# Feature pieces of a three-product matmul: heads and tails of the tokens as one moving operand of 512 columns, the halves of the bank added at the eviction

## The chip, the cores and the metric

The kernel runs on one core of a Trainium2 chip. The metric is the device time of one execution in microseconds. Three executions of the kernel before took 2441.64, 2445.85 and 2447.97 us; the median is 2445.85.

## The reference

All values are fp32. A sequence of 256 tokens with 2048 features goes through two blocks. The first block has two layers; in each, the normalized tokens are projected by one wide matrix, and the columns feed three kinds of attention (A: 6 heads with a decay, B: 6 heads through a low rank, C: 4 heads that take the difference of two softmaxes), whose gated outputs are projected back and added:

```python
for l in range(DEPTH):                       # 2 layers
    h = _rms_norm(x, norm_g[l])
    proj = jnp.einsum('bsd,dn->bsn', h, w_in[l])
    (a_q, a_k, a_v, a_f, a_gate, b_cq, b_ckv, b_krope, b_gate,
     c_q, c_k, c_v, c_gate) = jnp.split(proj, IN_OFFSETS, axis=-1)
    a_out = _fox_attention(...) * jax.nn.silu(a_gate)
    b_out = _mla_attention(...) * jax.nn.silu(b_gate)
    c_out = ... * jax.nn.silu(c_gate)
    mixed = jnp.concatenate([a_out, b_out, c_out], axis=-1)
    x = x + jnp.einsum('bsm,md->bsd', mixed, w_out[l])
```

The second block modulates and normalizes the tokens, runs two banded attentions with 64-wide heads (`proj = h @ w_in[l]`, split into qa, ka, va, qb, kb, vb), projects back, and ends with a mixture of 32 experts that runs all experts' weights past the tokens.

## The kernel before, in words

**Weights.** The weights of the first block and of the second block's attention come in pieces of 1 MB (128 x 2048 fp32), through a ring of 5 raw buffers loaded by SP. Each piece is split in halves of 1024 columns: ScalarE rounds a half to the fp32r format (`w_head`, L778, L1659), VectorE subtracts it from the raw half to get the rest (`w_tail`, L1175, L1889). There are 3 split buffers, and both splits run two pieces ahead (AHEAD = 2). The tokens are split in the same way into `h_head` and `h_tail`, 16 tiles of 128 features x 256 tokens each. A product is the sum of three matmuls, head x head, head x tail, tail x head (`three`, L945 and L1776).

**Pieces.** A layer of the first block has 73 pieces: 16 token pieces (out: tokens x 512 features, the tokens stationary, 512 columns moving), then 18 feature pieces of the A heads (query, key, gate of each of 6 heads), the feature piece of the rotary key (`kr`), 4 pieces of the low-rank projections (`low`, `lowv`), 6 feature pieces for the B gates, 12 for the C heads (query, key, gate), 16 output pieces. A feature piece (L1001, L1802) has the weights stationary (16 tiles of 128 x 128) and the 256 tokens moving, so 48 matmuls of 256 columns into one PSUM bank, of which the columns 0 to 255 are used. There are 37 such pieces in a layer and 26 in the second block (2 `ka`, 8 each of `qa`, `qb`, `kb`), so 100 in all.

**Order.** Each engine walks one list of steps, in strict order (`layer_schedule`, `second_schedule`); a piece is followed by steps due a number of pieces later. After an A key come its score and softmax, one piece later the transposes of the probabilities (`turn`), two pieces later the product with the values (`value`). After a B gate piece come the score of that B head, the gate and the softmax; after a C key two scores. In the second block the score follows `qa` (A part) or `kb` (B part), and the value step of the head before stands between the piece and the score. TensorE's score waits until the query and key of its head are evicted.

**Evictions.** In the first block VectorE evicts queries, keys and the rotary key: one instruction multiplies the bank by the tokens' reciprocal norms `rrow` (L1223 with a scale, L1226). For a gate VectorE multiplies (L1241), clamps (L1242), ScalarE takes exp, ln, exp (L875 to L877), and VectorE multiplies the result with the clamped value (L1246). In VectorE's order a gate of a B head stands after the reduction of the score (L1325 to L1332) and before its softmax (L1338 to L1341); in ScalarE's order it stands after the exponentials of the score (L902, L904). In the second block ScalarE evicts the feature pieces with one copy (L1707). 

**Beside it.** VectorE also sums the modulation weights (`ada`, L1262, 128 x 2048, about 2.35 us each), one after each of 16 in 18 pieces of a layer, and splits the mixed rows before the output pieces (L1386). Every wait is a counted semaphore; `chain.link` lets an instruction wait for the one before it on its own engine.

## Time and profile before

| | |
|---|---|
| median of three runs | 2445.85 us (2441.64 to 2447.97) |
| the profiled execution | 2444.84 us |
| its span, first to last instruction | 2442.7 us |
| mean granted TensorE clock | 0.977 of full speed |
| TensorE busy (matmuls) | 2222.4 us |
| VectorE busy | 1388.2 us |
| ScalarE busy | 732.9 us |
| HBM read | 757.28 MB, 311 GB/s over the span |

The rows below come from one profiled execution. A row of the timeline gives the start in us from the beginning of the span, the duration, the engine, the line of the kernel, the operation, what it writes and reads, its shape, and how many instructions the row holds. A bracket gives the idle time of the engine just before and the instruction that ended it; "issue" there means that the profile shows no releaser. PE is TensorE, PEld its weight load, DVE VectorE, ACT ScalarE. Matmuls are pipelined: their recorded durations overlap, so the distance between starts tells the pace. The first layer of the first block spans about 60 to 500 us, its A heads 136 to 264, B heads 288 to 355, C heads 355 to 443; the second layer repeats it about 500 us later; the feature pieces of the second block lie between 1062 and 1317 us, and the experts come after.

### The profile page before, as it was taken

How to read it: one execution, taken by the hardware profiler on the slowest of the kernel's cores; microseconds unless marked ns; L12 is line 12 of the kernel's file. 1: busy time of each engine (PE TensorE's matmuls, PEld its weight loads, DVE VectorE, ACT ScalarE, POOL GpSimd, SP SyncE). 2: the span in 40 equal slices, each digit the busy share in tenths (PEclk: the TensorE clock that was granted, in tenths of full speed). 3: DMA queues.
4: the chain of work that ended last, by engine and by line, in shares of the span. 5: the costliest groups of instructions: out<-in, count | busy, mean ns of one | idle time of the engine just before them, and what ended most of it. 6: DMA issues, size and time to landing. Idle time of an engine off the chain costs nothing. (4 is left out here: it accounts for less than half of the span.)

```text
span 2442.7 us, 37024 instructions
## 1 busy us (share of the span) xinstructions
PE 2222.4 (91%) x14593; PEld 1639.7 (67%) x14593; DVE 1388.2 (57%) x2051; ACT 732.9 (30%) x1343; POOL 43.0 (2%) x61
## 2 busy tenths in 40 slices
PE   6999999999999989979999978998888888888886
PEld 5899988788899888778898864444444444444442
DVE  6877788887787888666454634333333333333334
ACT  5444444454435434356554422000000000000001
POOL 0100000000000000030000000000000000000000
PEclk9999999999999999989999979999999999999998
DMA  8877766788777567674344256999999999999997
GB/s 320 322 298 292 275 242 247 307 314 338 293 295 274 224 260 265 246 269 148 147 141 152 105 227 245 422 422 422 422 422 422 422 422 422 422 422 422 422 422 322
DMA packets 108686, 761.77 MB, mean 312 GB/s; under 512 B 12288, under 2 KB 15392, under 8 KB 16800
## 3 DMA queue, kind: packets, MB, share of 16 engines
q1 hardware_dynamic: 108432, 759.49, 78.3%
q8 instruction: 73, 1.20, 0.2%
q10 hardware_dynamic: 144, 0.79, 0.1%
q14 instruction: 37, 0.30, 0.0%
HBM read 757.28 MB, written 2.95 MB: 311 GB/s over the span
## 5 line engine op out<-in xcount | busy, mean ns | idle before, releaser
L2312 PE MATMUL b_ps<-s_raw,s_window 128*64 128x256 f32 x4096 | 461.2, 382 | 58.2 <-DVE x_tokens L2538 39.3
L2312 PEld LDWEIGHTS b_ps<-s_raw,s_window 128*64 128x64 f32 x4096 | 295.6, 137 | 235.4 <-issue 72.6
L1175 DVE TENSOR_TENSOR s_w_tail<-s_raw,s_w_head 128x1024 fp32r<-128x1024 f32 x292 | 344.9, 1223 | 39.1 <-ACT s_w_head L778 39.0
L947 PE MATMUL b_ps<-s_h_head,s_w_head 128*128 128x256 f32 x1184 | 346.1, 292 | 0.0
L948 PE MATMUL b_ps<-s_h_tail,s_w_head 128*128 128x256 f32 x1184 | 339.1, 286 | 0.0
L949 PE MATMUL b_ps<-s_h_head,s_w_tail 128*128 128x256 f32 x1184 | 338.7, 286 | 0.0
L778 ACT ACTIVATE s_w_head<-s_raw 128x1024 fp32r<-128x1024 f32 x292 | 293.0, 1049 | 102.3 <-DMA s_raw<-in_w 70.6
L1262 DVE SCALAR_TENSOR_TENSOR s_ada_acc<-s_raw,s_c_col,s_ada_acc 128x2048 f32<-128x2048 f32 x120 | 282.3, 2352 | 0.0
L2332 PE MATMUL b_ps<-s_raw,s_diag 128*64 128x512 f32 x1024 | 237.8, 600 | 39.2 <-DMA s_raw<-in_w_down 24.0
L947 PEld LDWEIGHTS b_ps<-s_h_head,s_w_head 128*128 128x128 f32 x1184 | 231.1, 195 | 12.9 <-issue 9.4
L948 PEld LDWEIGHTS b_ps<-s_h_tail,s_w_head 128*128 128x128 f32 x1184 | 231.3, 195 | 0.2
L949 PEld LDWEIGHTS b_ps<-s_h_head,s_w_tail 128*128 128x128 f32 x1184 | 231.1, 195 | 0.0
L2220 ACT ACTIVATE s_hidden<-b_ps 128x256 f32<-128x256 f32 x32 | 12.3, 384 | 644.3 <-PE b_ps L2312 644.3
L2332 PEld LDWEIGHTS b_ps<-s_raw,s_diag 128*64 128x64 f32 x1024 | 66.1, 136 | 190.3 <-issue 84.8
L2530 DVE TENSOR_TENSOR s_y<-b_ps,s_gate_row 128x512 f32<-128x512 f32 x64 | 44.3, 692 | 237.4 <-PE b_ps L2332 237.4
L2538 DVE TENSOR_TENSOR x_tokens<-b_ps,x_tokens 128x1024 f32<-128x1024 f32 x128 | 147.8, 1217 | 32.5 <-PE b_ps L2347 32.5
L947 PE MATMUL b_ps<-s_w_head,s_h_head 128*128 128x512 f32 x416 | 164.2, 395 | 0.0
L949 PE MATMUL b_ps<-s_w_head,s_h_tail 128*128 128x512 f32 x416 | 162.8, 391 | 0.0
L948 PE MATMUL b_ps<-s_w_tail,s_h_head 128*128 128x512 f32 x416 | 162.8, 391 | 0.0
L1889 DVE TENSOR_TENSOR s_w_tail<-s_raw,s_w_head 128x1024 fp32r<-128x1024 f32 x104 | 126.3, 1253 | 54.1 <-ACT s_w_head L1659 53.9
L1778 PE MATMUL b_ps<-s_h_head,s_w_head 128*128 128x256 f32 x416 | 119.7, 288 | 0.9 <-ACT s_v L1697 0.9
L2516 DVE TENSOR_SCALAR s_hidden<-s_hidden 128x256 f32<-128x256 f32 x32 | 9.4, 294 | 193.1 <-ACT s_hidden L2220 193.1
(336 smaller groups left out, 3147.8 us busy)
## 6 DMA issues: line engine op xcount, KB each, us to landing
s_raw<-in_w SPq DMA_DIRECT2D x198, 1024.0 KB, 5.1
s_raw<-in_w_ada SPq DMA_DIRECT2D x128, 1024.0 KB, 5.2
s_raw<-in_w_gate SPq DMA_DIRECT2D x128, 1024.0 KB, 24.1
s_raw<-in_w_up SPq DMA_DIRECT2D x128, 1024.0 KB, 26.5
s_raw<-in_w_down SPq DMA_DIRECT2D x128, 1024.0 KB, 26.5
x_tokens<-in_x SPq DMA_DIRECT2D x1, 2048.0 KB, 7.8
s_rel<-in_rel SPq DMA_DIRECT2D x1, 2048.0 KB, 11.6
s_raw<-mod_rows SPq DMA_DIRECT2D x2, 1024.0 KB, 12.3
```

The source lines that it names most:

```text
L778: act.activation(w_head[:, g % SPLITS, cols], raw[:, ring, cols], ACT.Copy)\
L947: pe.matmul(out, head, m_head, start=first, stop=False, skip_group_check=True)
L948: pe.matmul(out, head, m_tail, start=False, stop=False, skip_group_check=True)
L949: return pe.matmul(out, tail, m_head, start=False, stop=last, skip_group_check=True)
L1175: dve.tensor_tensor(w_tail[:, g % SPLITS, cols], raw[:, slot["w", g], cols], w_head[:, g % SPLITS, cols].bitcast(F32), ALU.subtract)\
L1262: ins = dve.scalar_tensor_tensor(out=ada_acc[:, :], in0=raw[:, ring, :], scalar=c_col[:, 2, k:k + 1], in1=ada_acc[:, :], op0=ALU.mult, op1 ...
L1778: pe.matmul(out, head, m_head, start=first, stop=False, skip_group_check=True)
L1889: dve.tensor_tensor(w_tail[:, i % SPLITS, cols], raw[:, i % RAW, cols], w_head[:, i % SPLITS, cols].bitcast(F32), ALU.subtract)\
L2312: ins = pe.matmul(psum[64 * h:64 * h + 64, c // 4, 0:T], window[:, 4 * (c % 4) + k, :], raw[:, c, k * 512 + h * T:k * 512 + h * T + T], st ...
L2332: ins = pe.matmul(psum[rows_n, 4 + n % 2, :], hidden_t[:, m_ % 2, 64 * (m_ // 2):64 * (m_ // 2) + 64], raw[:, 8 + m_, n * 512:(n + 1) * 51 ...
L2530: dve.tensor_tensor(y[:, b, :], psum[:, 4 + b, :], gate_row[:, b, :], ALU.mult)\
L2538: dve.tensor_tensor(xs, psum[:, bank:bank + 2, :], xs, ALU.add).then_inc(sem["x_added"], 1)
```

## The change

The tokens' heads and tails are placed side by side in one buffer, tile by tile, `h_both[:, k, 0]` the head and `h_both[:, k, 1]` the tail. A feature piece does two matmuls per tile instead of three: the weights' head against all 512 columns (head and tail of the tokens), into the whole bank, and the weights' tail against the 256 columns of the head, into the first half. So the first half of the bank holds two of the products and the second half the third. At the eviction ScalarE first copies the second half to where the result goes, and counts `half_moved`; VectorE waits for that, adds the first half, and then does what it did before, now on its own result. For a gate the copy goes into the gate's slot, in ScalarE's step of that gate. In the second block ScalarE's former eviction becomes the copy (with its scale), and VectorE gets a new step after each feature piece, a fused multiply-add. Token, output and low-rank pieces and the experts keep their matmuls.

```diff
-    h_head = sb("h_head", [P, KT, T], F32R)
-    h_tail = sb("h_tail", [P, KT, T], F32R)
+    h_both = sb("h_both", [P, KT, 2, T], F32R)
+    h_head, h_tail = h_both[:, :, 0, :], h_both[:, :, 1, :]
...
@@ ScalarE, first block, piece and gate @@
+                    elif what == "feat" and s[3] in ("aq", "ak", "cq", "ck", "kr"):
+                        out = rope[:, 3, :] if s[3] == "kr" else qk[:, s[4] % 2, 0 if s[3][1] == "q" else 1, :]
+                        act.activation(out, full(act, s[2:], l)[:, T:2 * T], ACT.Copy).then_inc(sem["half_moved"], 1)
...
+                    gs = gate[:, gate_slot(ev, l), :]
+                    act.activation(gs, full(act, ev, l)[:, T:2 * T], ACT.Copy).then_inc(sem["half_moved"], 1)
                     freed(act, ev, l)
-                    gs = gate[:, gate_slot(ev, l), :]
                     chain.link(act.activation(gs, gate_raw[:, :], ACT.Exp, scale=-1.0))
...
@@ TensorE, both blocks @@
-                            ins = three(ps[:, 0:T], wh[:, k * P:(k + 1) * P], wt[:, k * P:(k + 1) * P],
-                                        h_head[:, k, :], h_tail[:, k, :], k == 0, k == KT - 1)
+                            pe.matmul(ps[:, :], wh[:, k * P:(k + 1) * P], h_both[:, k, :, :], start=k == 0,
+                                      stop=k == KT - 1, skip_group_check=True)
+                            ins = pe.matmul(ps[:, 0:T], wt[:, k * P:(k + 1) * P], h_head[:, k, :], start=False,
+                                            stop=k == KT - 1, skip_group_check=True)
...
@@ VectorE, first block @@
+                        dve.wait_ge(sem["half_moved"], at("half_moved", ev, l))
+                        chain.link(dve.tensor_tensor(out, ps[:, 0:T], out, ALU.add))
                         if name[1] == "q":
-                            dve.scalar_tensor_tensor(out=out, in0=ps[:, 0:T], scalar=(128 if name[0] == "a" else 64) ** -0.5, in1=rrow[:, :], op0=ALU.mult, op1=ALU.mult)\
+                            dve.scalar_tensor_tensor(out=out, in0=out, scalar=(128 if name[0] == "a" else 64) ** -0.5, in1=rrow[:, :], op0=ALU.mult, op1=ALU.mult)\
                                .then_inc(free_sem(ev, l), 1)
                         else:
-                            dve.tensor_tensor(out, ps[:, 0:T], rrow[:, :], ALU.mult).then_inc(free_sem(ev, l), 1)
+                            dve.tensor_tensor(out, out, rrow[:, :], ALU.mult).then_inc(free_sem(ev, l), 1)
...
                     ps = full(dve, ev, l)
-                    chain.link(dve.tensor_tensor(gate_raw[:, :], ps[:, 0:T], rrow[:, :], ALU.mult))
+                    dve.wait_ge(sem["half_moved"], at("half_moved", ev, l))
+                    chain.link(dve.tensor_tensor(gate_raw[:, :], ps[:, 0:T], gate[:, g, :], ALU.add))
+                    chain.link(dve.tensor_tensor(gate_raw[:, :], gate_raw[:, :], rrow[:, :], ALU.mult))
                     dve.tensor_scalar(gate_raw[:, :], gate_raw[:, :], -43.0, None, ALU.max)\
...
@@ second block: ScalarE, then VectorE @@
-                    act.activation(dst[:, t % 2, :], ps[:, 0:T], ACT.Copy,
-                                   scale=0.125 if name[0] == "q" else 1.0).then_inc(free_sem(ev), 1)
+                    act.activation(dst[:, t % 2, :], ps[:, T:2 * T], ACT.Copy,
+                                   scale=0.125 if name[0] == "q" else 1.0).then_inc(sem["half_moved"], 1)
...
+                if what == "feat":
+                    ev = s[2:]
+                    dve.wait_ge(sem["half_moved"], at("half_moved", ev))
+                    dst = {"qa": q_sb, "qb": q_sb, "ka": ka, "kb": kb}[s[3]][:, s[4] % 2, :]
+                    dve.scalar_tensor_tensor(out=dst, in0=full(dve, ev)[:, 0:T],
+                                             scalar=0.125 if s[3][0] == "q" else 1.0, in1=dst,
+                                             op0=ALU.mult, op1=ALU.add).then_inc(free_sem(ev), 1)
```

## Rows read from the trace of the kernel before

**Rows 1.** the page's busy times of each engine, share of the span, instructions
```profile
PE 2222.4 (91%) x14593; PEld 1639.7 (67%) x14593; DVE 1388.2 (57%) x2051; ACT 732.9 (30%) x1343; POOL 43.0 (2%) x61
```

**Rows 2.** stretches: length; busy PE, PEld, DVE, ACT, POOL; PEclk, DMA, GB/s
```profile
136.00:264.00 128.00, 125.05 (x960) 118.17 (x957) 98.36 (x141) 51.36 (x85) 0.00 (x0) 0.99 0.76 286
288.00:355.00 67.00, 65.92 (x479) 59.41 (x477) 56.25 (x113) 31.61 (x65) 0.00 (x0) 1.00 0.62 226
355.00:443.00 88.00, 76.61 (x582) 71.67 (x581) 72.09 (x143) 38.15 (x77) 0.00 (x0) 0.97 0.70 259
1062.00:1317.00 255.00, 250.26 (x1890) 227.74 (x1889) 142.03 (x341) 138.38 (x305) 18.11 (x16) 0.99 0.43 157
```

**Rows 3.** PE timeline: first and last matmul of two unbroken runs
```profile
300.11 0.28 PE L949 MATMUL b_ps<-s_h_head,s_w_tail 128*128 128x256 f32 x1
302.27 0.28 PE L949 MATMUL b_ps<-s_h_head,s_w_tail 128*128 128x256 f32 x1
...
100.03 0.39 PE L947 MATMUL b_ps<-s_w_head,s_h_head 128*128 128x512 f32 x1
102.97 0.39 PE L948 MATMUL b_ps<-s_w_tail,s_h_head 128*128 128x512 f32 x1
```

**Rows 4.** A heads: start us, duration, engine [idle before <-releaser]
```profile
184.35 0.42 DVE L1226 TENSOR_TENSOR s_qk<-b_ps,s_rrow 128x256 f32<-128x256 f32 x1 [0.39 <-PE b_ps L949]
184.88 0.46 PE L1092 MATMUL b_ps<-s_qk 128*128 128x128 f32 x2 [0.56 <-issue]
193.37 0.49 ACT L912 ACTIVATE s_p_t<-b_ps 128x384 f32<-128x384 f32 x1 [2.41 <-PE b_ps L1105]
194.58 0.42 DVE L1241 TENSOR_TENSOR s_gate_raw<-b_ps,s_rrow 128x256 f32<-128x256 f32 x1
195.03 0.29 DVE L1242 TENSOR_SCALAR s_gate_raw<-s_gate_raw 128x256 f32<-128x256 f32 x1
199.94 0.42 DVE L1223 SCALAR_TENSOR_TENSOR s_qk<-b_ps,s_rrow 128x256 f32<-128x256 f32 x1
205.46 0.42 DVE L1226 TENSOR_TENSOR s_qk<-b_ps,s_rrow 128x256 f32<-128x256 f32 x1 [0.23 <-PE b_ps L949]
...
228.05 0.42 DVE L1226 TENSOR_TENSOR s_qk<-b_ps,s_rrow 128x256 f32<-128x256 f32 x1 [0.80 <-PE b_ps L949]
```

**Rows 5.** timeline of one B head, from one tail split to the next
```profile
321.12 2.35 DVE L1175 TENSOR_TENSOR s_w_tail<-s_raw,s_w_head 128x1024 fp32r<-128x1024 f32 x2
...
326.75 0.42 DVE L1241 TENSOR_TENSOR s_gate_raw<-b_ps,s_rrow 128x256 f32<-128x256 f32 x1
326.87 0.40 ACT L902 ACTIVATE s_s_buf<-s_s_buf,s_stat 128x128 f32<-128x128 f32 x1 [4.47 <-DVE s_stat L1332]
327.77 0.40 ACT L875 ACTIVATE s_gate<-s_gate_raw 128x256 f32<-128x256 f32 x1
329.10 0.42 DVE L1246 TENSOR_TENSOR s_gate<-s_gate,s_gate_raw 128x256 f32<-128x256 f32 x1 [1.60 <-ACT s_gate L877]
330.10 2.35 DVE L1175 TENSOR_TENSOR s_w_tail<-s_raw,s_w_head 128x1024 fp32r<-128x1024 f32 x2
330.24 0.55 PE L1105 MATMUL b_ps<-c_sb,s_s_buf 128*128 128x128 f32 x3
```

**Rows 6.** timeline of the C heads and of the first output pieces
```profile
380.71 1.01 PE L1092 MATMUL b_ps<-s_qk 64*128 64x128 f32 x8 [1.71 <-issue]
...
424.88 0.43 DVE L1226 TENSOR_TENSOR s_qk<-b_ps,s_rrow 128x256 f32<-128x256 f32 x1 [1.85 <-PE b_ps L949]
...
442.09 0.76 PE L947 MATMUL b_ps<-s_w_head,s_low_head 128*128 128x512 f32 x1 [3.38 <-DVE s_h_tail L1386]
```

**Rows 7.** timeline of one head of the second block
```profile
1119.46 0.28 PE L1780 MATMUL b_ps<-s_h_head,s_w_tail 128*128 128x256 f32 x1
1119.84 0.38 ACT L1707 ACTIVATE s_q<-b_ps 128x256 f32<-128x256 f32 x1 [2.89 <-PE b_ps L1780]
1120.48 0.50 PE L1846 MATMUL b_ps<-s_ka,s_q 64*128 64x128 f32 x4
```

More of the change, by code:

```diff
@@ L533, in first_block @@
             tally.add("sigmoid", s[2:], l)
+        if kind == "gate":
+            tally.add("half_moved", s[1], l)
+        elif kind == "piece" and s[2] == "feat" and s[3] in ("aq", "ak", "cq", "ck", "kr"):
+            tally.add("half_moved", s[2:], l)
     at = tally.at
@@ L1514, in second_attention @@
             tally.add("m_tail", s[1])
+        elif kind == "piece" and s[2] == "feat":
+            tally.add("half_moved", s[2:])
         elif kind == "piece" and s[2] == "out" and s[4] == 3:
@@ L1528, in second_attention @@
     w_tail = sb("w_tail", [P, SPLITS, CHUNK_ELEMS], F32R)
-    h_head = sb("h_head", [P, KT, T], F32R)
-    h_tail = sb("h_tail", [P, KT, T], F32R)
+    h_both = sb("h_both", [P, KT, 2, T], F32R)
+    h_head, h_tail = h_both[:, :, 0, :], h_both[:, :, 1, :]
     mixed = sb("mixed", [P, KT, T])
@@ L1807, in _ @@
                             halves.second(ins)
-                        ins = three(ps[:, 0:T], wh[:, k * P:(k + 1) * P], wt[:, k * P:(k + 1) * P],
-                                    h_head[:, k, :], h_tail[:, k, :], k == 0, k == KT - 1)
+                        pe.matmul(ps[:, :], wh[:, k * P:(k + 1) * P], h_both[:, k, :, :], start=k == 0,
+                                  stop=k == KT - 1, skip_group_check=True)
+                        ins = pe.matmul(ps[:, 0:T], wt[:, k * P:(k + 1) * P], h_head[:, k, :], start=False,
+                                        stop=k == KT - 1, skip_group_check=True)
                     ins.then_inc(full_sem(ev), 1)
```

## The prediction

> **What bounds the kernel now.** I read the page first, for who is busy. TensorE is, for 91% of the span [rows 1], so a change that gives TensorE less to do looks like a gain. But that share averages over stages, so next come the busy times by stretch. In the stretches with the feature pieces of the first block's heads TensorE is busy 98% of the A heads' stretch (125.05 of 128 us) and VectorE 77% (98.36), in the B heads' 98% and 84% (56.25 of 67), in the C heads' 87% and 82% (72.09 of 88) [rows 2]. In the second block VectorE has room: 142.03 of 255 us. A VectorE busy for more than 80%, in strict order with waits inside its order, can be the bound while TensorE looks full, since matmuls are pipelined and their recorded times overlap. So the third view is the timeline, one head of each kind, looking for who waits for whom.
>
> A heads: VectorE reaches the eviction of a key piece 0.23 us before the piece is full (205.46) and TensorE then idles 0.56 us before the score matmuls (184.88), which need that eviction. From 184.35 to 205.46 is a head: 21.11 us [rows 4]. TensorE bounds it, and VectorE is 0.23 us behind being the bound itself. B heads: between the tail splits at 321.12 and 330.10, 8.98 us, VectorE runs without a hole but for one, 1.60 us, in which it waits for ScalarE's three sigmoid steps; the transposes (PE, 330.24) follow its softmax, which ends with the split's start. VectorE bounds these. C heads: TensorE idles 1.71 us before the scores at 380.71, and VectorE sat through no such wait there; it is the bound until the last head, where it waits 1.85 us for TensorE (424.88). After that TensorE waits 3.38 us for VectorE's last split of the mixed rows (442.09) [rows 6]. Second block: the piece's last matmul ends at 1119.74, ScalarE evicts by 1120.22, and the score begins at 1120.48, after the value matmuls that stand between: TensorE bounds, with 0.26 us to spare [rows 7].
>
> **What TensorE gains.** A run of 256-column matmuls starts one every 0.120 us (2.16 us over 18), a run of 512-column ones every 0.2262 (2.94 over 13) [rows 3]. A triple costs 0.360 us now; one of 512 and one of 256 make 0.3462 if each keeps its pace beside the other. That is 0.0138 per triple, 0.22 per piece of 16, and 22 us over the 100 feature pieces (37 in each of two layers, 26 in the second block), if all of it reached the end. The columns stay 768; what goes is one start. 
> **What is added.** ScalarE copies the second half of the bank (0.38 us, the eviction of rows 7, starting 0.10 after the last matmul). VectorE adds the first half (a 256-wide operation on PSUM, 0.42) and, in the first block, multiplies in a second step that waits for the add: a linked pair starts 0.45 apart (194.58, 195.03) [rows 4]. So a key, query or gate costs VectorE 0.45 more, and an eviction that TensorE waits for comes 0.10 + 0.38 + 0.45 = 0.93 later. An added step can be worth anything from 0.29 (the cheapest 256-wide step there, L1242) to 0.45; I take 0.45, the same kind of operation.
> [...] In the trace the product of two SBUF operands (L1246, 329.10) takes 0.42, as the one from PSUM does (L1241) [rows 5]. [...]
>
> **A heads, 12.** Three evictions per head add 1.35 us to VectorE's cycle, which without its wait for TensorE is 21.11 - 0.23 = 20.88: 22.23. The copies are there in time: for the gate ScalarE is free after the copy of 193.37, and VectorE comes at 194.58; for the query VectorE comes at 199.94, behind its split [rows 4]. TensorE's cycle becomes 21.11 - 3 x 0.22 + 0.93 = 21.38. VectorE is the later one: +1.1 for each of the 7 intervals of 21.11 (ten between heads, five a layer; the other three are 22.6, as 205.46 to 228.05, where the mean granted clock of the stretch is 0.99 and VectorE waits 0.80). Those three go by TensorE: +0.3 each. The first head of each layer: 0.93 - 0.22 = +0.7. The last gate and the rotary key piece, exposed nowhere: -0.22 each, four. Sum: 7.7 + 0.9 + 1.4 - 0.9 = **9 us**.
>
> **B heads, 12.** The gate is where ScalarE's new copy hurts: it stands behind the score's exponentials in ScalarE's order (326.87 to 327.77), while the multiply and the clamp (L1241, 326.75, and what follows) now run beside them for nothing. After the change VectorE can only begin once the copy ends, then add, multiply and clamp, and only then ScalarE's sigmoid begins, which now begins at 327.77: 0.38 + 0.03 + 0.45 + 0.45 + 0.29 + 0.03 = 1.63 us later (0.03 is a handover, the step from 195.00 to 195.03) [rows 4, 5]. Behind the waiting VectorE stand the softmax, hence TensorE's transposes, and the tail split of the next piece. TensorE, done 0.22 sooner, only waits longer. 12 x 1.63 = **20 us**. Bounds: 1.3 with the cheapest step, 1.8 with handovers of 0.10.
>
> **C heads, 8.** VectorE-bound from the B heads on up to the third key: eight evictions a layer, 16 x 0.45 = 7.2. The last head goes by TensorE: 2 x (0.93 - 0.66) = 0.5. The last gate stands ahead of the mixed split that TensorE waits for (442.09): 2 x 0.45 = 0.9 [rows 6]. Sum: **9 us**. The transfers of the weights wait for tail splits, and so come no earlier; they have room, the DMA share being 0.62 and 0.70 [rows 2].
>
> **Second block, 26 pieces.** ScalarE's eviction becomes the copy, and VectorE's fused multiply-add follows (0.03 + 0.42). Ready at 1120.67 instead of 1120.22, and 0.11 from there to the score, as 184.77 to 184.88: +0.30 for each of the 16 heads, against 0.22 for each of 26 pieces [rows 4, 7]: 4.8 - 5.7 = **-1 us**. VectorE waits in its order, but nothing that is due stands behind it there. The expert stage, the token and output pieces are untouched.
>
> **The sum.** 9 + 20 + 9 - 1 = +37 us on the profiled execution's own 2444.84 (span 2442.7 and 2.1 around it), 2482; that execution lies 1.0 below the median of the three runs, so 2482 to 2483. I say **2482**.
>
> **The rivals.** (1) *TensorE stays the bound and the waits stay exposed.* It needs VectorE's waits to shrink when its work grows. The gain of 22 then meets 20 key evictions at 0.93 and 16 at 0.30, 23.4: +1, 2447. Against it is the unbroken VectorE run of rows 5. Chance 0.05.
> (2) *Faster:* the copies run on an idle ScalarE and the adds fall into VectorE's holes (23% of the A heads' stretch is idle [rows 2]), so that only the second block's 4.8 is paid: 2445 - 22 + 5 = 2428. It decides where VectorE's cycle per head is under TensorE's; in the A heads that is a matter of 0.23 us, in B it is already lost. For it stands only the 91% of the page. Chance 0.05.
> (3) *The clock.* TensorE now waits longer at 36 places. A slow interval of the A heads costs 1.5 us (22.59 against 21.11 [rows 4]). In the B and C heads TensorE's slack absorbs it. If every interval of the A heads and every head of the second block got one, it would be 7 x 0.7 + 16 x 1.5 = 29 more: 2511. Against it: the waits before such intervals were 0.56 us and become about 1.5, where the C heads already have 1.7. Chance 0.1.
> (4) *The wide matmul saves nothing:* 10 us more, 2492; 0.1, inside the range. The case forecast has 0.7.
>
> **How the numbers follow.** With the cheapest step (0.29) the A and C heads lose about 6 us and B 4 less: 2472; a copy that now and then finds its place takes it to 2466. Upwards: no TensorE gain (2492), the 1.8 of the B heads (+2), a few slow intervals: 2500. What a measurement of this kernel can tell from no change is 0.3%, 7 us. Faster 0.05 (rival 2), same 0.05 (rival 1), slower 0.9.
>
> **What would show it.** Right: B heads 10.6 us apart, VectorE's wait before the gate's product still about 1.3 but a new one of about 1.3 before the add, TensorE idle some 1.7 us before the transposes; A heads 22.2 apart with no wait of VectorE for TensorE at the key; the TensorE start-to-start pattern 0.226 and 0.120. Wrong: a head interval below 21.1 in the A heads, B heads under 9 us, or an idle TensorE whose releaser is a DMA or ScalarE's weight split.

## The result and the profile after

The kernel after takes 2495.88 us (median of four runs, 2489.57 to 2503.53), against 2445.83 us for the kernel before on the same chip: a ratio of 1.0208 with an interval of 1.0176 to 1.024, 50 us slower. The forecast was 2482, in a range of 2466 to 2500. The profiled execution took 2495.97 us, its span 2493.9, at a mean granted TensorE clock of 0.968 (before 0.977).

The page's busy times and the two groups of the feature pieces' matmuls in the first block; they answer to [rows 1]. Fewer matmuls by 1600 as planned, yet TensorE is busy 10 us longer, VectorE 42.5 us longer:

```profile
PE 2232.5 (90%) x12993; PEld 1566.2 (63%) x12993; DVE 1430.7 (57%) x2151; ACT 756.6 (30%) x1417; POOL 42.8 (2%) x61
...
L1015 PE MATMUL b_ps<-s_h_both,s_w_head 128*128 128x512 f32 x1184 | 448.2, 419 | 0.0
L1017 PE MATMUL b_ps<-s_h_both,s_w_tail 128*128 128x256 f32 x1184 | 341.3, 288 | 0.0
```

**Where the time went.** The start of the scores is a mark that both kernels have at the same point of the work. The lag of the kernel after at these marks, and what each stretch added to it (both layers together; the two spans differ by 51.2):

| stretch, from score to score | forecast | measured |
|---|---|---|
| up to the first B score (A heads, rotary key, low-rank pieces) | +8.4 | 10.15 + 9.48 = +19.6 |
| first B score to first C score | +21.4 | 11.60 + 11.57 = +23.2 |
| C heads, first to last score | +5.9 | 4.71 + 2.28 = +7.0 |
| last C score to the next layer's first A score, or to the second block's first score | +1.6 | -1.73 - 2.00 = -3.7 |
| score steps of the second block, first to last | -1 | +1.3 |
| from there to the end | 0 | +3.9 |

(The forecast's terms are sorted by the same marks: two evictions of each layer's C heads lie ahead of the first C score, and the 0.7 for the second layer's first A head lies ahead of that layer's first A score.) The first line alone is 11.2 us over its forecast, where the whole sum was 14 us short.

The table compares one execution with one execution, and its lines are not equally firm. The second line is: the stretch took 63.55 and 63.57 us before, 75.14 and 75.15 after. The fourth is not: four versions traced below (eviction alone, early copy, filled waits, both remedies) have the same output pieces and the same evictions of queries and keys, and there it would read -1.5 to +1.6 instead of -3.7. The last is not either: that stretch took 1126.3 to 1132.1 us in the thirteen traces of this case, and the edits don't explain which.

**A heads.** Key and scores of one head, and the matmuls behind them, from the timeline. They answer to [rows 4]:

```profile
187.45 0.42 DVE L1233 TENSOR_TENSOR s_qk<-b_ps,s_qk 128x256 f32<-128x256 f32 x1
187.90 0.43 DVE L1238 TENSOR_TENSOR s_qk<-s_qk,s_rrow 128x256 f32<-128x256 f32 x1
188.43 0.46 PE L1102 MATMUL b_ps<-s_qk 128*128 128x128 f32 x2 [1.75 <-issue]
...
191.29 0.63 PE L1015 MATMUL b_ps<-s_h_both,s_w_head 128*128 128x512 f32 x1
191.72 0.41 PE L1017 MATMUL b_ps<-s_h_both,s_w_tail 128*128 128x256 f32 x1
191.93 0.63 PE L1015 MATMUL b_ps<-s_h_both,s_w_head 128*128 128x512 f32 x1
...
194.90 0.40 PE L1015 MATMUL b_ps<-s_h_both,s_w_head 128*128 128x512 f32 x1
195.13 0.28 PE L1017 MATMUL b_ps<-s_h_both,s_w_tail 128*128 128x256 f32 x1
...
197.37 0.40 PE L1015 MATMUL b_ps<-s_h_both,s_w_head 128*128 128x512 f32 x1
```

VectorE comes to the key without a bracket: it waits neither for TensorE nor for the copy, so it is the bound of this head, as forecast, and TensorE waits 1.75 us (0.56 before). Behind that wait a pair of matmuls takes 0.43 + 0.21 = 0.64 us from start to start, which is its 768 columns at the clock's lower level of 1.2 GHz; a few pairs later, at 2.4 GHz, seven of them take 197.37 - 194.90 = 2.47 us, 0.353 each. By stretch, from one score to the next (length; busy PE, PEld, DVE, ACT, POOL; PEclk, DMA, GB/s):

```profile
166.41:188.43 22.02, 20.27 (x112) 16.82 (x112) 18.63 (x28) 9.45 (x17) 0.00 (x0) 1.00 0.77 283
188.43:211.70 23.27, 21.54 (x111) 17.95 (x112) 18.76 (x28) 9.50 (x17) 0.00 (x0) 0.93 0.73 272
736.07:760.83 24.76, 23.06 (x112) 18.73 (x112) 18.77 (x28) 9.46 (x17) 0.00 (x0) 0.86 0.68 256
760.83:782.97 22.14, 20.27 (x111) 16.82 (x112) 18.67 (x28) 9.35 (x17) 0.00 (x0) 1.00 0.75 284
```

The heads at full clock stand 22.01 to 22.15 apart (forecast 22.23), but for the first interval of the second layer, 21.66. But five of ten intervals are slow, which here means that their mean granted clock is below 1.00: they take 23.2 to 24.8 us, where before three of ten were slow, at 22.6. The pieces behind the last A score ran slowly too: from there to the first B score it is 47.53 us in both layers, before 44.86 and 44.99.

**B heads.** They stand 10.73 us apart, before 8.98; the forecast was 10.6. One gate, from the timeline, answering to [rows 5]:

```profile
321.89 0.36 ACT L881 ACTIVATE s_gate<-b_ps 128x256 f32<-128x256 f32 x1
322.39 0.42 DVE L1254 TENSOR_TENSOR s_gate_raw<-b_ps,s_gate 128x256 f32<-128x256 f32 x1 [1.42 <-ACT s_gate L881]
322.85 0.42 DVE L1255 TENSOR_TENSOR s_gate_raw<-s_gate_raw,s_rrow 128x256 f32<-128x256 f32 x1
323.31 0.29 DVE L1256 TENSOR_SCALAR s_gate_raw<-s_gate_raw 128x256 f32<-128x256 f32 x1
323.63 0.42 ACT L883 ACTIVATE s_gate<-s_gate_raw 128x256 f32<-128x256 f32 x1 [1.38 <-DVE s_gate_raw L1256]
...
324.98 0.43 DVE L1260 TENSOR_TENSOR s_gate<-s_gate,s_gate_raw 128x256 f32<-128x256 f32 x1 [1.38 <-ACT s_gate L885]
```

VectorE waits 1.42 us for ScalarE's copy, which stands behind the exponentials, works through the gate, and waits 1.38 again for the sigmoid. TensorE idles 1.8 to 1.9 us before the transposes of the last three heads of each layer (forecast 1.7). Before, the add's place was taken by a multiply that ran beside the exponentials.

**C heads and the second block.** First the two C scores that answer to [rows 6], where TensorE waits 3.96 and 2.31 us (before 2.94 and 1.71), then a score of the second block with the copy, the added step and the wait for it, answering to [rows 7]:

```profile
379.85 1.74 PE L1102 MATMUL b_ps<-s_qk 64*128 64x128 f32 x8 [3.96 <-issue]
403.46 1.02 PE L1102 MATMUL b_ps<-s_qk 64*128 64x128 f32 x8 [2.31 <-issue]
...
1165.81 0.38 ACT L1723 ACTIVATE s_q<-b_ps 128x256 f32<-128x256 f32 x1 [2.79 <-PE b_ps L1826]
1166.23 0.42 DVE L1953 SCALAR_TENSOR_TENSOR s_q<-b_ps,s_q 128x256 f32<-128x256 f32 x1 [1.76 <-ACT s_q L1723]
...
1166.71 0.49 PE L1864 MATMUL b_ps<-s_ka,s_q 64*128 64x128 f32 x3 [0.18 <-DVE s_q L1953]
```

The score waits 0.18 us for VectorE, where it did not wait before. The heads there stand 13.82 to 14.04 apart in the A part (before 13.83) and 14.11 in the B part (before 14.01).

### The profile page after: what moved, and what is told of

Read it like the earlier page. It is cut to its first block and busy times, and to the rows that moved or that the text cites. A ratio compares the mean times of both kernels' runs of the same rounds, so it can differ in the third digit from the quotient of the medians.

```text
span 2493.9 us, 34067 instructions
## 1 busy us (share of the span) xinstructions
PE 2232.5 (90%) x12993; PEld 1566.2 (63%) x12993; DVE 1430.7 (57%) x2151; ACT 756.6 (30%) x1417; POOL 42.8 (2%) x61
## 5 line engine op out<-in xcount | busy, mean ns | idle before, releaser
L1015 PE MATMUL b_ps<-s_h_both,s_w_head 128*128 128x512 f32 x1184 | 448.2, 419 | 0.0
L1017 PE MATMUL b_ps<-s_h_both,s_w_tail 128*128 128x256 f32 x1184 | 341.3, 288 | 0.0
L1015 PEld LDWEIGHTS b_ps<-s_h_both,s_w_head 128*128 128x128 f32 x1184 | 233.8, 197 | 70.1 <-issue 12.8
L1017 PEld LDWEIGHTS b_ps<-s_h_both,s_w_tail 128*128 128x128 f32 x1184 | 234.9, 198 | 0.2
L955 PE MATMUL b_ps<-s_w_head,s_h_both 128*128 128x512 f32 x416 | 163.9, 394 | 0.0
L957 PE MATMUL b_ps<-s_w_head,s_h_both 128*128 128x512 f32 x416 | 162.5, 391 | 0.0
L956 PE MATMUL b_ps<-s_w_tail,s_h_both 128*128 128x512 f32 x416 | 162.5, 391 | 0.0
L1824 PE MATMUL b_ps<-s_h_both,s_w_head 128*128 128x512 f32 x416 | 149.0, 401 | 0.9 <-ACT s_v L1713 0.9
L2372 PE MATMUL b_ps<-s_y,s_weigh_t 64*128 64x512 f32 x512 | 118.5, 602 | 0.0
L1826 PE MATMUL b_ps<-s_h_both,s_w_tail 128*128 128x256 f32 x416 | 116.3, 280 | 0.0
```

The costliest lines, as they stand in the source:

```text
L955: pe.matmul(out, head, m_head, start=first, stop=False, skip_group_check=True)
L956: pe.matmul(out, head, m_tail, start=False, stop=False, skip_group_check=True)
L957: return pe.matmul(out, tail, m_head, start=False, stop=last, skip_group_check=True)
L1015: pe.matmul(ps[:, :], wh[:, k * P:(k + 1) * P], h_both[:, k, :, :], start=k == 0, stop=k == KT - 1, skip_group_check=True)
L1017: ins = pe.matmul(ps[:, 0:T], wt[:, k * P:(k + 1) * P], h_head[:, k, :], start=False, stop=k == KT - 1, skip_group_check=True)
L1824: pe.matmul(ps[:, :], wh[:, k * P:(k + 1) * P], h_both[:, k, :, :], start=k == 0, stop=k == KT - 1, skip_group_check=True)
```

## The experiments

The theory (T1) is the forecast's: the cost is the longer eviction in VectorE's order, most of it the place of ScalarE's copy in the B heads; the wide matmul by itself gains a little. All ratios are to the kernel before, measured beside it; its medians lay between 2443.8 and 2445.9.

### The two halves of the change apart

**The eviction alone.** The kernel after, its wide matmul taken apart again into two of 256 columns:

```diff
-                            pe.matmul(ps[:, :], wh[:, k * P:(k + 1) * P], h_both[:, k, :, :], start=k == 0,
+                            pe.matmul(ps[:, 0:T], wh[:, k * P:(k + 1) * P], h_head[:, k, :], start=k == 0,
+                                      stop=k == KT - 1, skip_group_check=True)
+                            pe.matmul(ps[:, T:2 * T], wh[:, k * P:(k + 1) * P], h_tail[:, k, :], start=False,
```

> The eviction of the changed kernel, but with three matmuls of 256 columns per tile: the head x tail product goes to the second half of the bank by a matmul of its own. Theory 1 (the eviction's chain through ScalarE and VectorE costs the time; the wide matmul hardly matters where VectorE bounds): as slow as the changed kernel or slower by what TensorE loses where it bounds, some 47 pieces at 0.15 us: 2495 to 2505 us, ratio to before 1.020 to 1.025; B heads 10.7 us apart. Theory 2 (the time is lost in the wide matmuls and the clock they leave): under 2460.

Measured: 2503.52 us, ratio 1.0239 [1.0226, 1.0252]. B heads 10.73 apart, A heads 22.05 to 22.16 at full clock and seven of ten slow.

**The wide matmul alone.** The kernel after with the old evictions, which read the first half of the bank only. It leaves out the product of the weights' heads with the tokens' tails in the feature pieces.

```diff
-                        dve.wait_ge(sem["half_moved"], at("half_moved", ev, l))
-                        chain.link(dve.tensor_tensor(out, ps[:, 0:T], out, ALU.add))
...
-                            dve.tensor_tensor(out, out, rrow[:, :], ALU.mult).then_inc(free_sem(ev, l), 1)
+                            dve.tensor_tensor(out, ps[:, 0:T], rrow[:, :], ALU.mult).then_inc(free_sem(ev, l), 1)
```

> The wide matmuls with the eviction of the kernel before: the second half of the bank, the product of the weights' head with the tokens' tail, is left out of the result of every feature piece. Theory 1: the gain of TensorE alone, 0.1 to 0.2 us a piece in the A heads, the last C head and the second block (some 70 pieces), nothing in the B heads: 2432 to 2440, ratio 0.994 to 0.998; B heads still 8.98 us apart. Theory 2: 2465 or more. If TensorE bounded everywhere the gain would be 22 us: 2424.

Measured: 2437.34 us, ratio 0.9973 [0.996, 0.9986]: 6.6 us gained. A heads 20.83 apart (21.11), B heads 8.97 (8.98), the second block 13.73 (13.83 and 14.01). Its page shows TensorE's busy time 12.9 us below the kernel before's [rows 1]:

```profile
PE 2209.5 (91%) x12993; PEld 1550.9 (64%) x12993; DVE 1387.1 (57%) x2051; ACT 731.9 (30%) x1343; POOL 46.0 (2%) x61
```

The two halves add up: 0.9973 x 1.0239 = 1.0211, the whole is 1.0208. The eviction costs 58 us and the matmul returns some 7 of them. Rival 4 (the wide matmul saves nothing) is out.

### The second block alone

The kernel before with the change of the second block (its matmuls, copy and added step) and nothing in the first.

> The change in the second block alone, the first block as before. Theory 1: 26 pieces gain 0.1 to 0.2 us, 16 heads wait 0.30 more for the score: between -1 and +2 us, ratio 0.9996 to 1.001, not to be told from no change. Rival: the second block carries a part of what the changed kernel lost beyond the forecast (some 14 us): 2455 or more.

Measured: 2447.28 us, ratio 1.0007 [0.9999, 1.0016], +1.7 us, which is not told from no change. The cost is in the first block.

### The place of the copy

ScalarE's copy of a gate moved from the gate's step, behind the score's exponentials, to the piece's step ahead of them:

```diff
+                    elif what == "feat":
...
+                        act.activation(gate[:, gate_slot(ev, l), :], full(act, ev, l)[:, T:2 * T], ACT.Copy)\
+                           .then_inc(sem["half_moved"], 1)
...
-                    act.activation(gs, full(act, ev, l)[:, T:2 * T], ACT.Copy).then_inc(sem["half_moved"], 1)
```

> The changed kernel with ScalarE's copy for a gate moved ahead of the exponentials of the score (into the step of the piece), nothing else. Theory 1: in the B heads add, multiply and clamp of the gate fall beside the exponentials again, so a B head falls from 10.73 to about 9.4 us, 12 x 1.3 = 16 us less than the changed kernel: 2480, ratio 1.014; A and C heads as in the changed kernel. Theory 2 (ScalarE's order does not matter, the amount of work does): 2496, ratio 1.021.

Measured: 2477.12 us, ratio 1.0145 [1.0121, 1.0169]. B heads 9.26 apart instead of 10.73. A gate of a B head in its timeline:

```profile
336.30 0.42 DVE L1255 TENSOR_TENSOR s_gate_raw<-b_ps,s_gate 128x256 f32<-128x256 f32 x1
336.39 0.40 ACT L911 ACTIVATE s_s_buf<-s_s_buf,s_stat 128x128 f32<-128x128 f32 x1 [4.24 <-DVE s_stat L1347]
...
337.55 0.42 ACT L884 ACTIVATE s_gate<-s_gate_raw 128x256 f32<-128x256 f32 x1 [0.17 <-DVE s_gate_raw L1257]
```

VectorE adds at once and beside the exponentials; its wait of 1.42 is gone, and the one at the gate's product (1.38) stays. Twelve gates at 1.47 us are 17.6 of the 18.8 us gained, and the stretches from the first B score to the first C score are indeed 8.8 us shorter in each layer. The six executions spread from 2470.18 to 2489.88 us, so the 18.8 alone would be a loose figure; the stretches are what hold it. So the place of one 0.36 us instruction in ScalarE's order cost some 18 of the 50 us.

### VectorE's load

**Short sums, before and after.** The sums of the modulation weights cut from 2048 columns to 16; both kernels leave out the rest of the sum.

```diff
-                        ins = dve.scalar_tensor_tensor(out=ada_acc[:, :], in0=raw[:, ring, :],
-                                                       scalar=c_col[:, 2, k:k + 1], in1=ada_acc[:, :],
+                        ins = dve.scalar_tensor_tensor(out=ada_acc[:, 0:16], in0=raw[:, ring, 0:16],
+                                                       scalar=c_col[:, 2, k:k + 1], in1=ada_acc[:, 0:16],
```

> The kernel before, with VectorE's 120 sums of the modulation weights in the first block cut from 2048 to 16 columns (so most of the modulation sums is left out of the result; loads, waits and order stay), which takes about 2.2 us a piece from VectorE. Theory 1: VectorE was the bound in the B and C heads, so it falls to TensorE's pace: C heads 21.1 apart instead of 22.6 and 23.6, no wait before the first C score, B heads 8.8: 2420 to 2432, ratio 0.990 to 0.994. Theory 2 (TensorE bounds everywhere): within 0.3% of before.

Before, cut: 2414.94 us, ratio 0.9881 [0.9866, 0.9896]. The gain of 29 us is more than the 12 to 24 expected. Its A heads are unchanged (21.11, TensorE's own pace), its C scores come 19.36 and 20.77 apart instead of 22.61 and 23.63 and wait for nothing, and 6.1 and 3.9 us more come from behind the last C score of each layer, which the expectation had left out.

> The changed kernel with the same cut of the modulation sums (again most of them left out of the result). Theory 1: with VectorE relieved the change costs only what TensorE still waits at the key evictions, 0.93 against 0.66 gained per head: 2 to 12 us more than the kernel before with that cut, where it is 50 with the whole sums: 2425 to 2440; A heads 21.4 apart (but for slow intervals), B heads 8.6. Theory 2 (the loss is TensorE's, its waits and its clock): 40 to 50 more than the kernel before with the cut.

After, cut: 2432.68 us, ratio 0.9957 [0.9943, 0.9971]. Of the 50 us, 17.7 are left (2432.68 - 2414.94). Between the two traces the B heads are level (8.72 against 8.81), and the C heads cost 4.0 us a layer. From the first A to the first B score it is 6.0 and 4.1 us: at full clock the A heads stand 21.56 to 21.78 apart (TensorE's own cycle with the longer key eviction, forecast 21.38; TensorE's wait at the key is 1.51 us instead of 0.56, and the 0.95 between them is the 0.93 of the forecast), and five of ten are slow (23.2 to 23.3) instead of three. So 32 of the 50 us hang on VectorE's load. The 18 of the copy's place are among them and not beside them: this kernel still has the copy in its late place, and with VectorE relieved its B heads lose nothing by it; the expectation's 2 to 12 for the rest was too low by TensorE's own waits and the clock behind them.

**The gate's last product on GpSimd.** To lighten VectorE without leaving out anything: the kernel before with only this moved, and the kernel after with this and the early copy.

```diff
+            for ev in gates:
+                g = gate_slot(ev, l)
+                freed(pool, ev, l)
+                pool.wait_ge(sem["sigmoid"], at("sigmoid", ev, l))
+                pool.tensor_tensor(gate[:, g, :], gate[:, g, :], gate_raw[:, :], ALU.mult).then_inc(sem["gate"], 1)
...
-                    dve.wait_ge(sem["sigmoid"], at("sigmoid", ev, l))
-                    freed(dve, ev, l)
-                    dve.tensor_tensor(gate[:, g, :], gate[:, g, :], gate_raw[:, :], ALU.mult)\
-                       .then_inc(sem["gate"], 1)
```

> The kernel before with the last product of each gate moved to GpSimd in the same way. Theory 1: the C heads lose VectorE's wait (22.6 and 23.6 fall to 21.1 and 21.9), B heads 8.8, A heads unchanged (TensorE bounds): 2428 to 2438, ratio 0.993 to 0.997, so the faster of the two kernels with this edit by some 10 us. Theory 2: no difference, 0.999 to 1.001.

Before: 2446.1 us, ratio 1.0007 [0.9998, 1.0016], no gain.

> The changed kernel with the early copy of the gates, and the last product of each gate (which VectorE does after a wait of 1.4 to 1.6 us for ScalarE) moved to GpSimd, 32 products of 128 x 256. Theory 1: VectorE's cycle loses 1.4 + 0.34 per gate, and TensorE bounds the A and B heads: A 21.4, B 8.6 apart, C still by VectorE at 21.1 to 23.2: 2442 to 2455, ratio 0.999 to 1.004. Theory 2 (amount of work, not waits): VectorE is relieved of 0.34 each, 11 us at most: 2466.

After: 2480.91 us, ratio 1.015 [1.0134, 1.0165], against 1.0145 [1.0121, 1.0169] without the move: no gain, and outside what either theory expected. The B heads of the kernel before did fall to the 8.8 forecast (8.81), but the wait ahead of the first C score grew from 2.94 to 3.93 us. The waits give both misses one explanation. First VectorE's waits in the C heads of the kernel before, then of the kernel before with the move (line, for what; us in total, times, longest):

```profile
DVE s_gate L1246 <- ACT s_gate L877: 4.3, 3, 1.4
...
DVE s_w_tail L1175 <- ACT s_w_head L778: 1.6, 3, 0.5
```

```profile
DVE s_w_tail L1179 <- ACT s_w_head L782: 7.2, 3, 2.4
```

(The windows run from 357 to 425 us.) ScalarE does the sigmoid and then the head of the next weights, and VectorE's tail split needs that head. Taking away the product and its wait only lengthens the next wait: 4.3 + 1.6 us of waits and three products of 0.42 became 7.2 of waits. GpSimd's product took 0.74 us. The kernel after shows the same exchange: in its B heads 6.9 us of waits for the sigmoid (early copy alone) became 6.7 us of waits for the head split (early copy and move), and the heads stand 9.20 instead of 9.26 apart. In the C heads, and in the B heads of the kernel after, ScalarE's order from the gate to the head split binds as well; VectorE's own instructions are not the whole of it, as I had taken them to be.

### The clock in the A heads

T1 here: TensorE's longer waits at the keys let its clock fall in the pieces behind. To test that, matmuls that nobody reads were put into the wait; they write into the score's bank before the scores do:

```diff
+                        ps = bank_for(pe, s, l)
+                        for _ in range(12):
+                            pe.matmul(ps[:, 0:T], h_head[:, 0, 0:P], h_head[:, 0, :], start=True, stop=True,
+                                      skip_group_check=True)
```

> The kernel after, with twelve extra matmuls of 256 columns (about 1.4 us) put where TensorE otherwise waits for the key of an A head, before the scores; they write into the score's bank, which the scores then overwrite. Theory 1 (TensorE's longer waits at the keys are what lets its clock fall in the pieces behind them): the slow intervals of the A heads (23.2 to 24.8 us in the kernel after) go or become fewer, the heads stand 22.1 to 22.4 apart since VectorE sets their pace and the extra matmuls lie in the wait, and the whole is 5 to 10 us shorter than the kernel after: 2486 to 2491, a ratio of 1.016 to 1.019. Theory 2 (the slow intervals have another cause, a state of the chip or the work of the interval itself): as many slow intervals as before, and no shorter: 2494 to 2500, or longer by what the extra matmuls delay.

Measured: 2490.44 us, ratio 1.0182 [1.0168, 1.0196], against 1.0208 [1.0176, 1.024] for the kernel after. The intervals of the ratios overlap; the timeline is clearer. The fill and the rest of the wait, and both layers' A heads from first to last score:

```profile
184.88 1.58 PE L1087 MATMUL b_ps<-s_h_both 128*128 128x256 f32 x12
187.02 0.46 PE L1106 MATMUL b_ps<-s_qk 128*128 128x128 f32 x2 [0.55 <-issue]
```

```profile
143.39:254.64 111.25, 109.14 (x618) 92.42 (x616) 90.29 (x135) 47.09 (x85) 0.00 (x0) 0.98 0.71 263
663.41:774.81 111.40, 109.43 (x617) 92.56 (x616) 90.37 (x135) 47.06 (x85) 0.00 (x0) 0.98 0.71 263
```

Two of ten intervals are slow instead of five, and the way from the last A score to the first B score is 44.4 us instead of 47.53. From the first A score to the first B score the two layers save 5.9 and 7.1 us against the kernel after. Of these 13 us the whole kept 5.4. The intervals between the A scores hold 6.8 of the 13, and these are what the fill can claim: five traces of versions with the long waits unfilled have five to seven slow intervals of ten (after, eviction alone, early copy, short sum, GpSimd). The other 6.2 lie in the way to the first B score, and there the kernel with the early copy, whose waits at the keys are as long and unfilled, takes 44.49 and 44.58 us too; that this part is the fill's doing is not shown.

> The kernel before, with four extra matmuls of 256 columns (about 0.5 us) in TensorE's wait of 0.56 us ahead of the scores of each A head. Theory 1 (the waits at the keys let the clock fall, in the kernel before too, only more seldom since they are shorter): its three slow intervals of ten (22.6 us) go, the heads stand 21.1 apart, and the whole is 2 to 5 us shorter: 2440 to 2443, a ratio of 0.998 to 0.999. Theory 2 (its slow intervals come from something else): the same number of them, 2445 to 2447, a ratio of 1.000 to 1.001.

The same in the kernel before, four matmuls: 2445.05 us, ratio 0.9998 [0.9988, 1.0007]. Its A heads show the clock as 1.00 throughout, and no interval is slow (three of ten before, where the two stretches took 107.02 and 108.54 us at 0.98 and 0.97; three, four and three in the other traces with the old evictions and waits of 0.56 us):

```profile
142.69:248.19 105.50, 105.06 (x818) 99.39 (x816) 84.33 (x120) 42.24 (x70) 0.00 (x0) 1.00 0.75 281
640.65:746.15 105.50, 105.07 (x817) 99.39 (x816) 84.41 (x120) 42.23 (x70) 0.00 (x0) 1.00 0.74 281
```

So the first part of T1 holds (the slow intervals go), and its sum does not: the profiled execution is 6.0 us ahead when the second block's scores begin, 4.5 when they end and 0.5 when the experts begin. The last stretch is in no way changed. The kernel before, then this one:

```profile
1315.51:1484.80 169.29, 138.86 (x632) 113.58 (x630) 89.54 (x179) 65.25 (x114) 2.40 (x7) 0.88 0.38 142
```

```profile
1311.04:1484.30 173.26, 141.75 (x632) 117.02 (x630) 89.49 (x179) 65.18 (x114) 2.39 (x7) 0.87 0.36 139
```

The same instructions take 4.0 us more. The kernel after has 172.85 there, the wide matmul alone 169.5. In the thirteen traces this stretch took either 168.8 to 169.5 us (seven of them) or 172.8 to 173.3 (six), and the two groups mix all edits: the kernel before with the short sums is in the long one, the kernel after with the same cut in the short one. So one execution's 4 us there say nothing on an edit. What makes an execution fall into the one or the other is open.

### Both remedies

> The kernel after with both remedies: ScalarE's copy of a gate ahead of the score's exponentials, and the twelve extra matmuls in the waits of the A heads. Theory 1 (the order of the copy in the B heads and the clock in the A heads are two separate costs, and what then remains is the 0.45 us that each of VectorE's 74 evictions got longer): the two savings add, 2477 less 5 to 8, so 2469 to 2472, a ratio of 1.010 to 1.011; it stays slower than the kernel before. Theory 2 (they overlap, or the clock falls elsewhere instead): 2475 to 2478, as with the early copy alone.

Measured: 2468.71 us, ratio 1.0101 [1.0086, 1.0117]. One A interval of ten is slow, the others 21.5 to 22.2; B heads 9.25 in the second layer. The remedies add (8.4 us less than the early copy alone), and 24.9 us of cost remain. No version tried that computes everything beats the kernel before.

## Why the prediction was right, and where it was short

The direction, the places and the mechanism held; the time came out 14 us above the forecast, inside the range, which was wide enough for two terms that were mis-sized, the clock's and TensorE's gain. Rivals 1 and 2 (both need TensorE to stay the bound) fall with the A heads, where VectorE no longer waits at the key, and with the 32 us that hang on VectorE's load; rival 4 falls with the wide matmul alone; rival 3, the clock, happened in part, beside the forecast's own terms.

- **What TensorE gains.** 0.22 per piece was too much. A pair takes 0.353 instead of 0.3462: the wide matmul starts 0.12 behind the small one and the small one 0.23 behind the wide one, but their sum runs at 0.35. Sixteen pairs save about 0.11. The wide matmul alone gives 0.09 per feature piece in the A heads ((21.11 - 20.83) / 3). The term for the second block changes sign with it: 4.8 - 26 x 0.11 is +1.9, and +1.7 was measured (not told from zero), -1 forecast. TensorE's cycle in the A heads becomes 21.71 instead of 21.38, which fits the 21.56 to 21.78 of the short sums.
- **A heads: VectorE's cycle.** 22.23 forecast, 22.01 to 22.15 measured at full clock (but for the one of 21.66), and VectorE waits at no A key but the first of each layer. This step was right.
- **A heads: the clock.** Here the forecast was short. It kept three slow intervals of ten and let them go by TensorE at +0.3 each, with nothing behind the last head; rival 3 stood at 0.1 with the argument that waits of 1.5 us are harmless since the C heads have 1.7. Measured were five slow intervals, 1.1 to 2.6 us over the full-clock pace, and 2.6 us more behind each last A score. Filling the waits removed most of the slow intervals; the part behind the last A score comes and goes between executions. The C heads' 1.7 was no evidence: TensorE has slack there, and a fall of its clock does not show in the distance of the scores. The first interval between C scores is 23.62 to 23.64 us in all twelve traced layers of the six versions with the change's evictions and full sums, while its mean granted clock ran from 0.86 to 0.93. In the table's first line the intervals are 5.3 us over their terms and the ways behind the last A scores 6.1, less 0.2 for the first head: 11.2.
- **B heads.** 1.63 forecast, 1.75 measured, from a wait of 1.42 for the copy (1.3 forecast) and 1.38 for the sigmoid; moving the copy returned 1.47 of it. Right, 1.8 us short over both layers.
- **C heads.** +7.0 measured, 5.9 forecast. The 0.45 per eviction is right in size: the four intervals that VectorE bounds grew by 1.01 to 1.33 us, three evictions each, 5.0 in all for 5.4 forecast. The last interval of each layer, which goes by TensorE, changed by +2.4 and -0.4 for 0.27 forecast; its granted clock went from 1.00 to 0.91 in the one layer and from 0.87 to 0.91 in the other, so that part is the clock again. That moving work off VectorE there gains nothing shows that ScalarE's chain binds too; the added 0.45 per eviction cost time because for a gate it lies on that chain (ScalarE's sigmoid waits for it). For the queries and keys no run takes their share away alone.
- **After the C heads.** Forecast +1.6, measured -3.7, with the wait for the mixed split at 3.5 us (before 3.4 [rows 6]). The same stretches took 2.2 to 5.3 us longer in the four other versions named under the table, so the gain is this execution's and not the change's, and the term can't be judged from it.
- **From the second block's scores to the end.** +3.9 in the profiled pair, in a stretch that varies by nearly 6 us between kernels that are the same there.

**Start-to-start, and the source of the multiply.** The traces show 0.120 us from start to start of 256 columns [rows 3] and save 0.11 per piece. By the Trainium skill ("TensorE: Matmul & The Clock Gate", Back-to-back issue gap), with the 2.5 ns per start that it gives for an isolated matmul, a piece would save an estimated 0.04. The measurement lies between that and my 0.22, nearer the first. The table of the Trainium skill ("VectorE: DVE Perf Modes", The TRN2 errata) gives a VectorE operation 58 cycles besides its elements when it reads SBUF and 120 when it reads PSUM, so, as an estimate from it, the multiply would have become 62 cycles cheaper by moving to SBUF. The rows show no difference either way: the add reading the bank took 0.42 and the multiply reading only SBUF 0.42 or 0.43, and the measurement decides.

## What to carry to other kernels

A saved instruction start on the engine that looks full is worth what the stretches where that engine truly binds can collect (7 us here), and a step added to the eviction is paid wherever the evicting engine binds (58 us). Before adding a helper instruction on an idle engine, look at what stands ahead of it in that engine's order: here its place cost some 18 us. Before calling a few us the effect of an edit, look whether other traces have the same stretch without that edit: here three stretches moved by 3 to 6 us on their own. Price a wait of TensorE not only by its length but by the slow matmuls behind it, and by the stretches where no slack hides them.

## What the runs showed of the hardware

- Behind a wait of 1.75 us four pairs in a row (191.29 to 193.85) ran at 0.64 instead of 0.353 us, and the granted clock of that interval was 0.93. Slow intervals of ten in one traced execution each: with the waits of 0.56 us of the old eviction three, four, three and three (before, second block alone, short sum, GpSimd); one in the wide matmul alone, with waits of 0.56 to 0.78; none with the wait filled to 0.09; with unfilled waits mostly of 1.5 to 2.1 us five to seven in five versions, and two and one where the fill left 0.1 to 0.7 of them.
- The spread between executions of one kernel goes with the clock: in 17 executions of the kernel before the spans run from 2439.6 us at a mean granted clock of 0.979 to 2449.3 us at 0.974.
- Three matmuls of 256 columns keep 0.120 us from start to start also when they alternate between the two halves of the bank (the eviction-alone kernel). Its timeline:

```profile
176.02 0.28 PE L1015 MATMUL b_ps<-s_h_both,s_w_head 128*128 128x256 f32 x1
176.14 0.28 PE L1017 MATMUL b_ps<-s_h_both,s_w_head 128*128 128x256 f32 x1
176.26 0.28 PE L1019 MATMUL b_ps<-s_h_both,s_w_tail 128*128 128x256 f32 x1
```

- GpSimd multiplies 128 x 256 fp32 in SBUF in 0.74 us (mean of 32, by records that are rough for this engine), where VectorE takes 0.42.
